# A two-layer stack and a hybrid layer on one core: the second value product halved among the attention jobs, and the norm steps of a mixer at fixed rounds

## The reference

```python
# layer 0: MoBA heads (8) and NSA heads (8); layer 1: 16 heads with forget gates
h = h + moba_nsa_mixer(rmsnorm(h, g0), w_in, w_out, rel_bias, ...)   # "even"
h = h + sqrelu_mlp(rmsnorm(h, m0), w1, w2)
h = h + fox_mixer(rmsnorm(h, g1), w_in, b_forget, w_out)             # "odd"
h = h + sqrelu_mlp(rmsnorm(h, m1), w1, w2)
x = rmsnorm(h, final_norm)
# hybrid layer
x = x + 0.5 * rms_norm(swiglu(rms_norm(x, ..), ..), ffn1_post_g)
proj = rms_norm(x, mix_pre_g) @ w_in          # q, k, v, z, xbc, dt
o = softmax(q1 k1 + bias) v - lam * softmax(q2 k2 + bias) v          # 8 heads of 64
attn = rms_norm(o, subln_g) * (1 - lambda_init)                      # per head
y = ssd_chunked(silu(conv(xbc)), ...) + xs * d_skip                  # 16 heads of 64
ssm = rms_norm((y * silu(z)).reshape(2 groups of 512), norm_g)       # per group
x = x + rms_norm(concat(attn, ssm) @ w_out, mix_post_g)
x = x + 0.5 * rms_norm(swiglu(...), ffn2_post_g)
```

## Time and profile before

| what | us |
|---|---|
| median of the runs | 1239.46 |
| lowest and highest run | 1237.42, 1242.24 |
| profiled execution, its time | 1237.19 |
| its span (first to last instruction) | 1235.4 |
| PE busy | 1192.0 (96%) |
| mean granted clock of PE | 0.995 |

### The profile page before, as it was taken

One profiled execution on the slowest core, in us unless ns is written; L12 is line 12 of the kernel. 1 busy time (PEld: TensorE's weight loads), 2 busy tenths in 40 slices (PEclk: granted clock), 3 DMA queues, 4 the chain that ended last, 5 costly groups with the idle time before them and its releaser, 6 DMA issues.

```text
span 1235.4 us, 19213 instructions
## 1 busy us (share of the span) xinstructions
PE 1192.0 (96%) x7770; PEld 1046.7 (85%) x7770; DVE 825.7 (67%) x1267; ACT 658.1 (53%) x1074; POOL 236.0 (19%) x300
## 2 busy tenths in 40 slices
PE   7898999999999999999999999999999899999996
PEld 6786788888888688888888889999997698888996
DVE  5957776666586686675657777457865757667643
ACT  6428666643343756664346655336546754655531
POOL 4104421210000431220012222000004511212101
PEclk9999999999999999999999999999999899999999
DMA  7791245455444335455544554652451122455451
GB/s 281 253 240 35 102 171 197 181 202 204 173 171 194 148 105 202 174 201 205 190 171 153 202 182 152 205 213 105 171 205 69 35 103 104 170 197 178 158 196 56
DMA packets 33800, 205.56 MB, mean 166 GB/s; under 512 B 3744, under 2 KB 6320, under 8 KB 12720
## 3 DMA queue, kind: packets, MB, share of 16 engines
q1 hardware_dynamic: 30416, 200.47, 45.4%
q10 hardware_dynamic: 3296, 3.87, 1.6%
HBM read 202.87 MB, written 1.46 MB: 165 GB/s over the span
## 4 chain that ended last, share of the span: by engine, by line
PE 77%; DVE 13%; ACT 5%; DMA 2%; issue 1%; ACTq 0%; POOL 0%; POOLq 0%; DVEq 0%
PE ps L669 36%; PE ps L674 23%; PE ps L672 5%; PE ps L673 5%; DVE wl L611 4%; DMA e_bt<-scratch 2%; DVE tf L2228 1%; ACT wh L582 1%; PE ps L693 1%; PE ps L695 1%; PE ps L694 1%; DVE y L1949 1%; ACT pb L924 1%; DVE xb L747 1%; ACT pb L923 1%
## 5 line engine op out<-in xcount | busy, mean ns | idle before, releaser
L611 DVE TENSOR_TENSOR wl<-raw,wh 128x2048 fp32r<-128x2048 f32 (+2 forms) x194 | 420.4, 2172 | 148.3 <-ACT wh L582 148.3
L669 PE MATMUL ps<-xb,wh 128*128 128x512 f32 x1424 | 500.7, 397 | 4.6 <-DVE wl L611 4.1
L674 PE MATMUL ps<-xb,wl 128*128 128x256 f32 x1696 | 475.6, 280 | 0.0
L582 ACT ACTIVATE wh<-raw 128x2048 fp32r<-128x2048 f32 (+2 forms) x196 | 352.1, 1799 | 151.1 <-PE ps L674 112.9
L669 PEld LDWEIGHTS ps<-xb,wh 128*128 128x128 f32 x1424 | 267.3, 188 | 70.3 <-issue 5.7
L674 PEld LDWEIGHTS ps<-xb,wl 128*128 128x128 f32 x1696 | 321.6, 190 | 0.0
L674 PE MATMUL ps<-ab,wl 128*128 128x256 f32 x1088 | 305.7, 281 | 0.0
L669 PE MATMUL ps<-ab,wh 128*128 128x512 f32 x640 | 225.1, 397 | 0.1
L674 PEld LDWEIGHTS ps<-ab,wl 128*128 128x128 f32 x1088 | 206.4, 190 | 0.0
L669 PEld LDWEIGHTS ps<-ab,wh 128*128 128x128 f32 x640 | 120.1, 188 | 29.2 <-DVE ab L982 0.8
L866 DVE TENSOR_TENSOR tf<-ps,tf 128x256 f32<-128x256 f32 x148 | 61.8, 421 | 117.7 <-ACT tf L861 117.5
(11 more groups left out here) (324 smaller groups left out, 1324.7 us busy)
## 6 DMA issues: line engine op xcount, KB each, us to landing
raw<-wstream SPq DMA_DIRECT2D x162, 1024.0 KB, 4.8
raw<-wstream SPq DMA_DIRECT2D x32, 704.0 KB, 4.1
e_bt<-scratch ACTq DMA_DIRECT2D x16, 128.0 KB, 8.8
o_bt<-scratch SPq DMA_DIRECT2D x2, 1024.0 KB, 9.9
raw<-wstream SPq DMA_DIRECT2D x2, 560.0 KB, 8.8
raw<-wstream SPq DMA_DIRECT2D x4, 256.0 KB, 6.5
h<-xt ACTq DMA_DIRECT2D x4, 256.0 KB, 7.7
raw<-wstream SPq DMA_DIRECT2D x2, 512.0 KB, 9.7
```

Of the source, the lines that this page charges most:

```text
L582: e.g.activation(WH[i % HLN][:, 0:w], RAW[i % RAWN][:, 0:w], ACT.Copy).then_inc(S["hi"], 1)
L611: e.g.tensor_tensor(WL[q][:, 0:w], RAW[i % RAWN][:, 0:w], f32(WH[q][:, 0:w]), ALU.subtract).then_inc(S["lo"], 1)
L669: e.g.matmul(PS[b][:, :].rearrange("p (a t) -> p a t", a=2), wh[:, sl], x2[:, :, cs], start=start, stop=k == p.nk - 1, skip_group_check=pair)
L674: ins = e.g.matmul(o, wl[:, sl], xh[:, cs], start=False, stop=k == p.nk - 1, skip_group_check=pair)
```

## The change

1. **Even attention.** `ev1` is cut by k: blocks 0 to 3 in PE's turn 2, blocks 4 to 7 in turn 5, into banks 1 and 0, where the value product of job 0 goes afterwards. ACT copies the next chunk's high half alone at i = 2, ahead of exp(2), and moves `ev1` out at i = 5. DVE's `lo_to` goes from i = 3 to i = 5. `dve_even_gates` becomes three pieces: sums at i = 1 and 2, gates at 6 and 7, weights at 8 and 9 (with a semaphore `pcs` between).
2. **Odd attention.** `ov1` is cut in the same way, halves in turns 2 and 5 and not ahead of job 0. ACT's copy of the chunk behind it goes to i = 3, DVE's to i = 4, the quarters of the chunk after that from i = 1, 3, 5, 7 to 7, 9, 11, 13 on ACT and from 8 to 11 to 14 to 17 on DVE.
3. **Mixer.** DVE's late steps stand at fixed places. In round 5 two `normed` go ahead of the reciprocals, two behind them; the head norm of tile 0 moves from the end of round 5 to round 6, behind `weighted(7)` and ahead of the reciprocals. The low halves of the first y tiles go to rounds 6 and 7. The quarters of `mo`'s chunk stand at i = 1 (two), 2 and 3, none at 4. ACT's high half of tile 0 comes a round later. In MIXK tile 0 comes behind 6 and 7, and the weights are packed so; in round 7 PE begins one tile and in round 8 three.

```diff
-MIXK = [4, 5, 0, 6, 7, 1, 8, 9, 2, 10, 11, 3]
+MIXK = [4, 5, 6, 7, 0, 1, 8, 9, 2, 10, 11, 3]
...
-        Gemm("ev1", "toks", 280, 8, 4, "ev_act"),
+        Gemm("ev1", "toks", 280, 8, 4, "ev_act", fixed=(1, 0)),
-        Gemm("ov0", "toks", 512, 8, 4, "ev_act"), Gemm("ov1", "toks", 512, 8, 4, "ev_act"),
+        Gemm("ov0", "toks", 512, 8, 4, "ev_act", fixed=(5, 6)), Gemm("ov1", "toks", 512, 8, 4, "ev_act", fixed=(1, 0)),
...
-        def pe_toks(e, p, ready):
+        def pe_toks(e, p, ready, part=slice(None)):
 
             w = p.nt
-            for _, k, c, at, fresh, signals in p.blocks:
+            for _, k, c, at, fresh, signals in p.blocks[part]:
...
-                    act_exp_biased(e, A, 2)
-                    act_exp_biased(e, A, 3)
+                    hi_to(e, G["eo"].first)
+                if i == 5:
+                    act_exp_biased(e, A, 5)
                     act_gemm(e, G["ev1"], drain=act_toks(G["ev1"], e_v, 512, 0), ahead=1)
...
-                if i < A.n and i not in (2, 3):
+                if i < A.n and i != 5:
...
-                if i in (7, 9):
-                    dve_even_gates(e, i // 9)
+                if i in (1, 2):
+                    dve_even_sums(e, i - 1)
+                if i in (6, 7):
+                    dve_even_gates(e, i - 6)
+                if i in (8, 9):
+                    dve_even_weights(e, i - 8)
...
-                if i == 3:
+                if i == 5:
+                    dve_reciprocal(e, A, 3)
+                    dve_turned(e, A, 1)
                     lo_to(e, G["eo"].first)
-                if 0 <= i - 1 < A.n:
+                if 0 <= i - 1 < A.n and i != 4:
                     dve_reciprocal(e, A, i - 1)
-                if 0 <= i - 3 < A.n and i % 2 == 0:
+                if 0 <= i - 3 < A.n and i % 2 == 0 and i != 4:
...
         def dve_even_gates(e, tb):
-            gz, ss = e_v[tb][:, 768:792], SMALL[:, 16 + tb * 8:24 + tb * 8]
+            gz = e_v[tb][:, 768:792]
             e.wait_ge(S["gz"], tb + 1)
             e.link(e.g.tensor_scalar(gz, gz, 1.0, None, ALU.add))
             e.settle()
             e.g.reciprocal(gz, gz).then_inc(S["gated"], 1)
+
+        def dve_even_sums(e, tb):
+
+            ss = SMALL[:, 16 + tb * 8:24 + tb * 8]
             e.wait_ge(S["pce"], tb + 1)
             e.link(e.g.tensor_reduce(ss, pcv[:, tb, :, 0:15], AX, ALU.add))
             e.settle()
-            e.link(e.g.reciprocal(ss, ss))
-            e.settle()
+            e.g.reciprocal(ss, ss).then_inc(S["pcs"], 1)
+
+        def dve_even_weights(e, tb):
+
+            ss = SMALL[:, 16 + tb * 8:24 + tb * 8]
+            e.wait_ge(S["pcs"], tb + 1)
             e.wait_ge(S["gated"], tb + 1)
...
-                if i == 2:
-                    pe_toks(e, G["ev1"], x_ready(0))
+                if i in (2, 5):
+                    pe_toks(e, G["ev1"], x_ready(0), slice(0, 4) if i == 2 else slice(4, 8))
...
-            act_gemm(e, G["ov1"], drain=act_toks(G["ov1"], o_v, 512, 2), ahead=1)
             A = ODD
             for i in range(A.n + 4):
-                if 1 <= i < 9 and i % 2:
-                    hi_part(e, G["oo"].first + 1, i // 2)
+                if 7 <= i < 15 and i % 2:
+                    hi_part(e, G["oo"].first + 1, (i - 7) // 2)
                 if i < A.n:
                     act_exp_biased(e, A, i)
+                if i == 3:
+                    hi_to(e, G["oo"].first)
+                if i == 5:
+                    act_gemm(e, G["ov1"], drain=act_toks(G["ov1"], o_v, 512, 2), ahead=1)
                 if 0 <= i - 3 < A.n and i % 2:
...
-            dve_gemm(e, G["ov1"], 0, ahead=1)
+            dve_gemm(e, G["ov1"], 0, ahead=0)
             A = ODD
             for i in range(A.n + 5):
-                if 8 <= i < 12:
-                    lo_part(e, G["oo"].first + 1, i - 8)
+                if 14 <= i < 18:
+                    lo_part(e, G["oo"].first + 1, i - 14)
+                if i == 4:
+                    lo_to(e, G["oo"].first)
...
-            pe_toks(e, G["ov1"], x_ready(2))
             A = ODD
             pe_odd_scores(e, 0)
             for i in range(A.n + 4):
+                if i in (2, 5):
+                    pe_toks(e, G["ov1"], x_ready(2), slice(0, 4) if i == 2 else slice(4, 8))
                 if i % 2 and i + 1 < A.n:
...
-                    elif kind == "sub" and step == 3:
+                    elif kind == "sub" and step == (3 if s else 4):
...
+            def head_norm(s):
+                oa = m_oa[:, tile(s)]
+                e.wait_ge(S["nb_y"], nb_no("sub", s))
+                e.link(rsqrt_dve(e, RT[:, 0:T], RT[:, T + 2:2 * T + 2], RB2[:, :]))
+                e.settle()
+                e.wait_ge(S["sbq"], s + 1)
+                e.g.scalar_tensor_tensor(out=oa, in0=oa, scalar=SMALL[:, 180:181], in1=RB2[:, :], op0=ALU.mult,
+                                         op1=ALU.mult).then_inc(S["om"], 1)
...
                 if i + 1 < 8:
                     weighted(i + 1)
+                if i == 5:
+                    normed(0, 1)
+                elif i == 6:
+                    head_norm(0)
+                elif i == 7:
+                    group_lows(2, 3)
...
+                if i == 4:
+                    group_factor(0)
+                elif i == 5:
+                    normed(2, 3)
+                elif i == 6:
+                    group_lows(0, 1)
+                elif i == 7:
+                    mixed_low(e, 0, m_oa[:, tile(0)])
+                    head_norm(1)
+                elif i == 8:
+                    group_factor(1)
+                    mixed_low(e, 1, m_oa[:, tile(1)])
...
-                if 1 <= i <= 4:
-                    lo_part(e, G["mo"].first + 2, i - 1)
+                if i == 1:
+                    lo_part(e, G["mo"].first + 2, 0)
+                if 1 <= i <= 3:
+                    lo_part(e, G["mo"].first + 2, i)
...
-                begun(*{7: (5, 0), 8: (6, 7), 9: (1,), 10: (8, 9), 11: (2,), 12: (10, 11, 3)}.get(i, ()))
+                begun(*{7: (5,), 8: (6, 7, 0), 9: (1,), 10: (8, 9), 11: (2,), 12: (10, 11, 3)}.get(i, ()))
```

59 lines of the change are left out of this document (30 added, 29 removed).

## The result

| | before | changed |
|---|---|---|
| median of the runs | 1238.97 us (6 runs) | 1230.15 us (6 runs) |
| lowest and highest | 1235.71, 1242.24 | 1226.23, 1230.88 |
| profiled execution, its span | 1235.4 | 1228.9 |
| its mean granted clock | 0.995 | 0.994 |

The ratio of changed to before is 0.9924, with a 95% interval of 0.9901 to 0.9948: 9.4 us faster, between 6.4 and 12.3 (the two medians lie 8.8 apart). The forecast was 1230.3.

The account below looks back on a forecast made before the run. PE was taken as the bound, busy 1192.0 of 1235.4 us. Gains of 2.0 (even attention), 2.2 (odd) and 5.0 (mixer), 9.2 in all, take the median from 1239.46 to 1230.3 us; whole range 1225.5 to 1236.5.

Parts of the forecast that it names:

- Even attention, 2.0: Even attention: moving lo_to and the gates' sums out of DVE's busy stretch gains 2.0 us, bounds 0 to 4.5.
- 2 x 0.45: Even attention: the gates' sums, about 2 x 0.45 us, leave DVE's busy stretch for turns 1 and 2.
- 0.7 in my walk: Even attention: job 0's value product newly waits some 0.7 us for ev1 to be moved out of its banks.
- Odd attention, 2.2: Odd attention: earlier job 0 scores remove 2.0 us of PE idle and about 0.2 of restarts; bounds 0.5 to 2.8.
- Mixer, 5.0: Mixer, rounds 5 to 7: 2.2 - 0.6 + 3.4 gives 5.0 us; upper bound 6.5, lower cases 1.6 and 1.0.
- 2.2 for the wait: Mixer: states of round 6 wait less for weighted(7), so scores of round 7 come 2.2 us earlier.
- 0.6 at the turns: Mixer: PE waits 0.6 us at round 6's turns, for reciprocals behind the head norm and POOL's diagonal.
- 3.4 for the clock: Mixer: without the 2.8 us idle PE stays at 2.4 GHz from 980 to 987 us, returning 3.4 us.
- The rule of the Trainium skill: Mixer: POOL can hold up two-input DVE instructions; head norm held at 3.0 us, pair of normed up to 0.5 more.
- rival (a): Mixer: the clock falls all the same, so the mixer gives 1.6 us and the time is 1233.7 us; chance 0.16.
- Rival (b): Attentions: the gaps only move, so even gives 0, odd 0.5, and the time is 1234.0 us; chance 0.14.
- rival (c): Attentions: a long bank wait at job 0's value product costs idle and clock, slower at 1246.9 us; chance 0.05.

Follow-up runs that it names:

- gates_only: Kernel before with only the gates cut into three pieces, ev1 whole: median 1240.19 us, ratio to before 0.9989 (0.9965 to 1.0012).
- no_gates: Changed kernel with the gates kept in one lump at jobs 7 and 9: median 1232.16 us, ratio to before 0.9949.
- whole_ev1: Changed kernel with ev1 whole in turn 2 and the next chunk's copies where before has them: median 1228.94 us, ratio to before 0.9919.
- odd_only: Kernel before with only the odd attention's part of the change: median 1236.63 us, ratio to before 0.9981 (0.9960 to 1.0001).
- mixer_only: Kernel before with only the mixer's part of the change: median 1233.57 us, ratio to before 0.9962 (0.9949 to 0.9975).
- head_back: Changed kernel with the head norm of tile 0 back at the end of round 5: median 1236.12 us, ratio to before 0.9945.
- even_only: Kernel before with only the even attention's part of the change: median 1235.92 us, ratio to before 0.9985 (0.9973 to 0.9998).
- again: Changed kernel, unedited, measured once more: median 1231.31 us, ratio to before 0.9915 (0.9883 to 0.9948).

## Why the prediction was right

**The sum.** Forecast 9.2, measured 9.4 (6.4 to 12.3), from parts of 2.0, 2.2 and 5.0 against 1.9, 2.4 and 4.7 alone. The places were right: PE's idle time goes in all three. The sum is in part luck. The term of the even attention was right for a reason other than its working, that of the odd one was 0.7 us too small by its stage, and that of the mixer comes to about 4.0 from its two steps where I had 5.0; the misses offset one another.

**Even attention, 2.0.** Right in size, wrong in the step. I counted `lo_to` out of the way of jobs 2 to 4 as the larger part, and the sums of the gates as 2 x 0.45 of it. The runs show the reverse: the pieces of the gates bring the 2 us, through the waits for DVE's maxima (1.1 us in all, gone in `gates_only`) and what follows from them, and the halving brings 0.1 to 0.4 with the lump (`no_gates`) and 0.1 without (`whole_ev1`). The lump was in plain view, 1.38 us ahead of job 7's maximum, twice, in a stretch in which PE's next scores waited for that maximum. The subtraction of 2.29 us holds back the reciprocal of job 2, and in the profile of before PE waits 0.97 us for the division behind it, the 1.0 of the earlier trace rows. In the four other profiles with the subtraction in its old place and `ev1` whole (`odd_only`, `mixer_only`, `gates_only`, `whole_ev1`) that wait isn't there: they have the low clock at 91 us, `ev1` takes longer at it, and the division is done in time. So moving the subtraction freed little in them. What the halving is worth without the low clock no run shows, since no profile of it lacks the stretch. The new wait for `ev1`'s banks, 0.7 in my walk, isn't there: ACT had moved `ev1` out at 103.46 + 0.88 = 104.3, ahead of the value product at 104.7 in the changed kernel, one with the low clock.

```profile
103.46 0.88 ACT L872 ACTIVATE e_v<-ps,rb 128x280 f32<-128x280 f32 x2 [0.77 <-PE ps L695]
...
104.68 0.65 PE L1488 MATMUL ps<-pt,e_v 128*64 128x256 f32 x4
```

**Odd attention, 2.2.** Right as worked: scores of job 0 behind `ov0`, the first maximum as soon as DVE has its chunk copies done, no idle on PE behind it. DVE in the changed kernel (shifted by 3.66 us against before, so the forecast of 400.0 reads 403.7 here):

```profile
401.41 2.29 DVE L611 TENSOR_TENSOR wl<-raw,wh 128x2048 fp32r<-128x2048 f32 x1 [0.17 <-ACT wh L582]
403.62 0.28 DVE L933 CUSTOM_DVE_ANT_0 pb<-ps,o_bt 128x128 f32<-128x128 f32 x1
```

The size was too small: the stage gives 2.9. PE's idle time of 2.0 is gone; the other 0.9, for which I had 0.2, is in PE's busy time, which over the stage goes from 41.93 to 40.91 us with the same 275 matmuls. I put it down to the restarts behind each wait, which cost PE more than the printed wait. That is argued and not shown.

**Mixer, 5.0.** The steps were 2.2 for the wait, less 0.6 at the turns, and 3.4 for the clock. Of profiles without low clock in the mixer, two with the long wait take 91.16 and 91.54 us there (`head_back`, `even_only`) and four with the short one of 0.7 us 90.03 to 90.09: 1.1 to 1.5 for the first two steps, where I had 1.6. The runs give about 2.7 for the clock, where I had 3.4. In all 4.0; the part alone measured 4.7 (3.1 to 6.3). Of the 1.5 us between the old mixer (91.54, `even_only`) and the new one, the place of the head norm is 1.1 (91.16 in `head_back`); all the other steps of part 3 together are 0.4 in these profiles. Inside, the wait of states is 0.7 and not nothing: `weighted(7)` took 0.91 us and not 0.58 beside POOL. The head norm, which I held at 3.0 for POOL's sake, took 1.8 and the turns didn't wait:

```profile
976.08 0.91 DVE L2323 TENSOR_TENSOR m_eb<-m_eb,m_cbt 128x384 f32<-128x384 f32 x1
976.91 0.41 DVE L802 TENSOR_TENSOR rt<-rb 128x256 f32<-128x256 f32 x1
977.36 0.43 DVE L804 SCALAR_TENSOR_TENSOR rt<-rt 128x256 f32<-128x256 f32 x1
```

POOL's last step, the square, had begun at 975.97 and took 0.61 us: `weighted` overlapped it, the head norm didn't. The instruction that is slowed is the one that stands there when POOL works, and the row told that there is a slowing but not where it would fall. The rule of the Trainium skill ("GPSIMD Engine Reference", key points) on the shared access to SBUF held, with 0.58 against 0.91 us, for another instruction than the one that I had charged with it.

**The clock.** That an idle of 2.8 us "set the clock down" was right as a tendency and too strong as a cause: two profiles with 2.5 us of it kept 1.00. Against rival (a) I held that gaps of about 1 us don't take the clock down, with the 1.00 of the even attention for it; the profile of before was the exception there, and in the mixer a gap of 0.95 us was followed by a low clock in the changed kernel's first profile. It was 3.4 us long and cost half of what (a) had (1.7 for 3.4), and `again` has none. So (a) came about in part in one execution and not in the time. Rival (b) held for the halving of `ev1`, without harm to the sum; rival (c), a long wait for the banks, not at all.

## What to carry to other kernels

Look for lumps of small instructions that stand, each waiting for the one before, ahead of something that the bound engine waits for: two of 1.38 us cost more here than a subtraction of 2.3 us whose delay other work covered in most profiles. When a profile has one stretch of low clock, ask whether other executions have it too: the mean clock of the timed runs tells, and a stage of one profile may be set against another's only with the low clock alike. A part that rides along in a change should be tried by itself; the most intricate one here, the halving of `ev1`, was worth 0.1 us in its own stage, and 0.6 in the next one through a wait that it wasn't made for.
